# A two-layer encoder trunk on one core: expert outputs summed in DRAM instead of gathered per choice

## The reference, cut to what matters

```python
for l in range(2):
    x = x + mixer(rmsnorm(x)) @ w_out[l]
    h2 = rmsnorm(x, norm2_g[l])
    # each token: best of 4 groups, then the best 2 of that group's 4 experts, with gates
    for e in range(16):            # SwiGLU experts, 1024 -> 512 -> 1024
        act = silu(h2 @ w_gate[e]) * (h2 @ w_up[e]) * gate[:, e]
        y += act @ w_down[e]       # gate is zero for all but 2 experts of a token
    x = x + y
return rmsnorm(x, final_g)
```

## Time and profile before

| | |
|---|---|
| median of 3 runs | 1093.71 us (1092.78 to 1094.87) |
| the profiled execution's own time | 1096.58 us |
| its span, first to last instruction | 1094.3 us |
| PE busy | 1034.2 us (95%) |
| DVE, ACT, POOL busy | 549.2, 291.3, 191.8 us |
| mean granted TensorE clock | 0.987 |
| moved by DMA | 279.07 MB, mean 255 GB/s |

### The profile page before, as it was taken

How to read it: one execution, slowest core, us unless ns; L and a number is a source line. 1 busy time by engine, 2 the same in 40 slices (tenths; PEclk the granted TensorE clock), 3 DMA queues, 4 the chain that set the end, 5 groups by cost and what they waited for, 6 DMA issues and landing times.

```text
span 1094.3 us, 26585 instructions
## 1 busy us (share of the span) xinstructions
PE 1034.2 (95%) x11288; PEld 765.1 (70%) x11288; DVE 549.2 (50%) x1264; ACT 291.3 (27%) x570; POOL 191.8 (18%) x265
## 2 busy tenths in 40 slices
PE   8999998899999999899989999989999999998894
PEld 7875874587689977586578577646876778764552
DVE  5899996524711111020679999764364112102018
ACT  6225336623000100000342443465230001000013
POOL 3400000000223442322200000000003335332230
PEclk9999999999999999999999999999999999999997
DMA  9652211153999999999934122011569999999993
GB/s 358 209 230 78 77 58 39 39 193 147 394 399 406 402 404 401 405 402 400 345 125 137 53 93 89 20 51 50 202 261 401 403 406 400 404 401 407 396 389 127
DMA packets 85109, 279.07 MB, mean 255 GB/s; under 512 B 12344, under 2 KB 12448, under 8 KB 84976
## 3 DMA queue, kind: packets, MB, share of 16 engines
q1 hardware_dynamic: 69504, 237.60, 56.8%
q0 software_dynamic: 15472, 39.63, 9.8%
HBM read 257.43 MB, written 22.54 MB: 256 GB/s over the span
## 4 chain that ended last, share of the span: by engine, by line
PE 64%; DVE 16%; DMA 10%; issue 3%; ACT 3%; SPq 3%; DVEq 0%; ACTq 0%
PE ps L861 20%; PE ps L901 9%; DVE arena L1620 7%; PE ps L459 7%; PE ps L461 7%; PE ps L460 7%; DMA deep<-in_w_dn 3%; DMA deep<-in_w_gu 3%; SPq L410 3%; DVE w_lo L440 2%; PE ps L906 2%; DMA arena<-in_w_dn 2%; DVE x_sb L1559 2%; DMA arena<-in_w_gu 2%; PE ps L1048 2%
## 5 line engine op out<-in xcount | busy, mean ns | idle before, releaser
L1839 DVE SCALAR_TENSOR_TENSOR arena<-ps,gslot,arena 128x128 f32<-128x128 f32 x88 | 25.7, 345 | 368.1 <-ACT arena L1259 333.2
L861 PE MATMUL ps<-arena 128*32 128x256 f32 x2112 | 129.6, 380 | 6.3 <-DMA arena<-in_w_dn 3.2
L640 POOL DMA_INDIRECT gain<-h_rows,tab x82 | 85.1, 1037 | 231.6 <-DVE arena L1831 188.9
L459 PE MATMUL ps<-a_hi,w_hi 128*128 128x512 f32 (+1 forms) x304 | 122.5, 403 | 3.1 <-DVE w_lo L440 2.1
L460 PE MATMUL ps<-a_lo,w_hi 128*128 128x512 f32 (+1 forms) x304 | 119.3, 392 | 0.0
L461 PE MATMUL ps<-a_hi,w_lo 128*128 128x512 f32 (+1 forms) x304 | 119.2, 392 | 0.0
L861 PEld LDWEIGHTS ps<-arena 128*32 128x32 f32 x2112 | 90.4, 110 | 39.2 <-issue 9.7
L861 PE MATMUL ps<-deep,arena 128*32 128x256 f32 x1824 | 106.6, 379 | 1.0 <-DMA deep<-in_w_dn 1.0
L861 PE MATMUL ps<-raw,arena 128*32 128x256 f32 x1696 | 103.2, 379 | 0.5
L435 ACT ACTIVATE w_hi<-raw 128x1024 fp32r<-128x1024 f32 (+1 forms) x64 | 65.0, 1022 | 131.1 <-PE ps L461 130.9
L1259 ACT ACTIVATE arena<-ps 128x384 f32<-128x384 f32 (+1 forms) x32 | 14.9, 465 | 315.3 <-PE ps L861 248.8
(11 more groups left out here) (266 smaller groups left out, 1511.7 us busy)
## 6 DMA issues: line engine op xcount, KB each, us to landing
arena<-in_w_gu SPq DMA_DIRECT2D x92, 512.0 KB
deep<-in_w_gu SPq DMA_DIRECT2D x84, 512.0 KB
raw<-in_w_gu SPq DMA_DIRECT2D x80, 512.0 KB
raw<-in_w_dn SPq DMA_DIRECT2D x56, 512.0 KB
deep<-in_w_dn SPq DMA_DIRECT2D x44, 512.0 KB
raw<-in_w_in SPq DMA_DIRECT2D x40, 512.0 KB
arena<-in_w_dn SPq DMA_DIRECT2D x28, 512.0 KB
raw<-in_w_out SPq DMA_DIRECT2D x16, 512.0 KB
```

Source lines behind the costliest of these rows:

```text
L459: nc.tensor.matmul(o, lh, rh, start=start, stop=False)
L640: pool.indirect_dma_start(xg[:, s * QC:(s + 1) * QC], None, h2q[l], bass.IndirectOffsetOnAxis(ap=tab[:, s, e:e + 1], axis=0), bounds_check ...
L861: mm = T.matmul(o, rows, piece[:, :, c * P:(c + 1) * P], start=b == 0, stop=b == 7)
L1839: ins = V.scalar_tensor_tensor(out=slu[:, s, :], in0=hidden(e, 1)[:, s, :], scalar=gslot[:, s, e:e + 1], in1=slu[:, s, :], op0=ALU.mult, o ...
```

## The change

Each finished seat is added to one DRAM row per token. `ysum` has one row of 4 KB per token for each layer, cleared at the start by eight DMAs of 512 KB (with one for the zero row, nine instead of twelve). `store` issues one indirect DMA per group, three or two instead of four plain ones; the offsets are the `tab` entries that the gather used, entries out of bounds are skipped, and the DMA adds to what the row holds. Since two seats can hold the same token, each store also waits on POOL until all earlier stores have landed. At the end four plain loads of 512 KB bring the summed rows, and DVE adds four tiles instead of eight. The table of result rows `yidx[:, 0]` and the DVE instructions that made it are gone; `stored` counts indirect DMAs.

```diff
+        ysum = [nc.dram_tensor(f"y_sums{l}", (SEQ, D), F32, kind="Internal").ap() for l in range(DEPTH)]
+        ysq = [rows.rearrange("t (q n) -> (t q) n", q=4) for rows in ysum]
...
+        def stored(l, e):
+            return TURNED[STORED] * l + TURNED[e]
...
-                            sp.wait_ge(yc_in[TT - 1], 32 * l)
+                            sp.wait_ge(yc_in[TT - 1], 16 * l)
...
-                    for tile in range(1 + EXTRA):
-                        pool.dma_start(yd[ZERO_ROW + tile * P:ZERO_ROW + (tile + 1) * P, :], zeros).then_inc(y_zero, 16)
+                    pool.dma_start(yd[ZERO_ROW:ZERO_ROW + P, :], zeros).then_inc(y_zero, 16)
+                    for rows in ysum:
+                        for tt in range(TT):
+                            pool.dma_start(rows[tt * P:(tt + 1) * P, :], zeros).then_inc(y_zero, 16)
...
                 def store(e):
                     pool.wait_ge(y_set, STORED * l + e + 1)
-                    rows = yd[FIRST_ROW[e]:FIRST_ROW[e + 1], :].rearrange("(s i) (c n) -> c i s n", i=G, c=4)
-                    for c in range(4):
-                        pool.dma_start(rows[c], ysb[G * c:G * c + G, 0:GROUPS_OF[e] * QC].rearrange("i (s n) -> i s n", n=QC)).then_inc(y_stored, 16)
+                    if e:
+                        pool.wait_ge(y_stored, 16 * stored(l, e))
+                    elif l == 0:
+                        pool.wait_ge(y_zero, 16 * (1 + DEPTH * TT))
+                    for s in range(GROUPS_OF[e]):
+                        pool.indirect_dma_start(ysq[l], bass.IndirectOffsetOnAxis(ap=tab[:, s, e:e + 1], axis=0), ysb[:, s * QC:(s + 1) * QC], None,
+                                                bounds_check=4 * SEQ - 1, oob_is_err=False, compute_op=ALU.add).then_inc(y_stored, 16)
...
-                if l == 0:
-                    pool.wait_ge(y_zero, 16 * (1 + EXTRA))
-                pool.wait_ge(y_stored, 64 * STORED * (l + 1))
+                pool.wait_ge(y_stored, 16 * stored(l, STORED))
                 for tt in range(TT):
-                    for k in range(TOPE):
-                        q = TOPE * tt + k
-                        if q == LATE_FREE:
-                            pool.wait_ge(w_used, (l + 1) * PIECES_L - 8)
-                        pool.indirect_dma_start(late_rows[q], None, yd,
-                                                bass.IndirectOffsetOnAxis(ap=yidx[:, 0, k, tt:tt + 1], axis=0)).then_inc(yc_in[tt], 16)
+                    pool.dma_start(late_rows[tt], ysum[l][tt * P:(tt + 1) * P, :]).then_inc(yc_in[tt], 16)
...
-                    sc.wait_ge(y_stored, 64 * (STORED * l + e))
+                    sc.wait_ge(y_stored, 16 * stored(l, e))
...
-                ve.wait_ge(yc_in[tt], 32 * (l + 1))
-                for k in range(TOPE):
-                    ve.wait_ge(late_add, TOPE * (TT * l + tt) + k)
-                    V.tensor_tensor(x[:, tt, :], late_rows[TOPE * tt + k], x[:, tt, :], ALU.add).then_inc(late_add, 1)
+                ve.wait_ge(yc_in[tt], 16 * (l + 1))
+                V.tensor_tensor(x[:, tt, :], late_rows[tt], x[:, tt, :], ALU.add).then_inc(late_add, 1)
...
-                link(V.tensor_scalar(R["v2"], e2k[:], float(-LIGHT.start), 0.0, ALU.add, ALU.max))
...
-                V.tensor_scalar(yidx[:, 0], R["c2"], float(ZERO_ROW), None, ALU.add)
```

More of the change, by code:

```diff
@@ L76 @@
 TURNED = [sum(GROUPS_OF[:p]) for p in range(E + 1)]
-FIRST_ROW = [sum(ROWS_OF[:p]) for p in range(E + 1)]
 EXTRA = 11
@@ L80 @@
 STORED = E - LAST
-ZERO_ROW = FIRST_ROW[STORED]
+ZERO_ROW = 0
 SUM_BANK = (2, 4, 6, 0)
@@ L191, in trunk @@
         warm = sb("warm", [P, 2 + 2 * DEPTH])
-        yidx = sb("yidx", [P, 2, TOPE, TT], I32)
+        yidx = sb("yidx", [P, TOPE, TT], I32)
         e2k = sb("e2k", [P, TOPE, TT])
@@ L261, in trunk @@
         SIDE_MIX, SIDE_ROWS = 6, 10
-        late_rows = [ar(A_ACC, D), ar(A_SQ, D), *(deep[:, d].rearrange("p a n -> p (a n)") for d in (3, 7)),
-                     ar(A_L, D), ar(A_PT, D), hrow[:, TT - 1, :], ar(A_V, D)]
-        LATE_FREE = 5
+        late_rows = [ar(A_ACC, D), ar(A_SQ, D), *(deep[:, d].rearrange("p a n -> p (a n)") for d in (3, 7))]
         at = A_SC
@@ L675, in _ @@
                 with pool.If(extra > 0):
-                    pool.wait_ge(late_add, TT * TOPE * (l + 1))
+                    pool.wait_ge(late_add, TT * (l + 1))
                     pool.wait_ge(over[l].tab_step, TABLES)
@@ L690, in _ @@
                         for tt in range(TT):
-                            pool.indirect_dma_start(x[:, tt, :], None, yd, bass.IndirectOffsetOnAxis(ap=yidx[:, 1, k, tt:tt + 1], axis=0),
+                            pool.indirect_dma_start(x[:, tt, :], None, yd, bass.IndirectOffsetOnAxis(ap=yidx[:, k, tt:tt + 1], axis=0),
                                                     compute_op=ALU.add).then_inc(over[l].xg_in, 16)
@@ L1554, in add_late @@
             def add_late(l, tt):
-                ve.wait_ge(yc_in[tt], 32 * (l + 1))
-                for k in range(TOPE):
-                    ve.wait_ge(late_add, TOPE * (TT * l + tt) + k)
-                    V.tensor_tensor(x[:, tt, :], late_rows[TOPE * tt + k], x[:, tt, :], ALU.add).then_inc(late_add, 1)
+                ve.wait_ge(yc_in[tt], 16 * (l + 1))
+                V.tensor_tensor(x[:, tt, :], late_rows[tt], x[:, tt, :], ALU.add).then_inc(late_add, 1)
             def sum_ready(l, tt):
-                ve.wait_ge(late_add, TOPE * (TT * l + tt + 1))
+                ve.wait_ge(late_add, TT * l + tt + 1)
                 ve.wait_ge(ysum_ready, TT * l + tt + 1)
@@ L1745, in extras @@
                     link(V.scalar_tensor_tensor(out=R["ex"], in0=R["count"], scalar=float(q), in1=R["ex"], op0=ALU.is_gt, op1=ALU.add))
-                link(V.tensor_scalar(R["v2"], e2k[:], float(-LIGHT.start), 0.0, ALU.add, ALU.max))
[L1747 to L1753, removed]
                 link(V.tensor_tensor_scan(R["cum"], cst[:, C_ONE:C_ONE + E], R["ex"], 0.0, ALU.mult, ALU.add))
-                link(V.scalar_tensor_tensor(out=R["c2"], in0=R["k2"], scalar=float(CAP), in1=R["c2"], op0=ALU.is_lt, op1=ALU.mult))
                 V.tensor_tensor(first_of[:], R["cum"], R["ex"], ALU.subtract)
                 V.tensor_copy(ovx[:, EXTRA:EXTRA + 1], R["cum"][:, E - 1:E])
-                link(V.scalar_tensor_tensor(out=R["c2"], in0=R["b2"], scalar=float(-ZERO_ROW), in1=R["c2"], op0=ALU.add, op1=ALU.mult))
-                V.tensor_scalar(yidx[:, 0], R["c2"], float(ZERO_ROW), None, ALU.add)
                 link(V.tensor_tensor(R["cmp"], R["cum"].unsqueeze(1).to_broadcast([P, EXTRA, E]),
@@ L1802, in over_rows @@
                 step(V.scalar_tensor_tensor(out=R["d2"], in0=R["b2"], scalar=float(OVER_ROW - ZERO_ROW - E * P), in1=R["d2"], op0=ALU.add, op1=ALU.mult))
-                V.tensor_scalar(yidx[:, 1], R["d2"], float(ZERO_ROW), None, ALU.add)
+                V.tensor_scalar(yidx[:], R["d2"], float(ZERO_ROW), None, ALU.add)
                 for k in range(TOPE):
@@ L1927, in _ @@
                 if l == 0:
-                    ve.wait_ge(y_zero, 16 * (1 + EXTRA))
+                    ve.wait_ge(y_zero, 16 * (1 + DEPTH * TT))
                 for v, (h, b) in enumerate(DOTS):
```

## The result

The changed kernel takes 1101.85 us (median of 6 runs, 1098.94 to 1104.14), the kernel before 1094.82 us in the same comparison (6 runs, 1092.78 to 1096.51): ratio 1.006, 95% interval [1.0045, 1.0075]. It is 7.0 us slower where 6.1 us less was forecast. The profiled execution took 1102.13 us with a span of 1100.2 us; the granted clock was 0.99, the same as before.

What follows compares the result with a forecast made beforehand. It took the DMA engines to bound the expert stages and DVE the layer ends; -7.2 us at the ends and +1.1 us for adding stores gave -6.1 us, 1093.71 becoming 1087.6 us, range 1079 to 1107.

Steps and rivals of the forecast that it cites:

- What bounds the kernel: Expert stages up to seat 13's last down weights: DMA engines set the pace, 2.49 us per MB paid nearly one for one.
- The ends of the layers: Last `last_y` to first `add_sum`: fewer DVE additions save 3.1 us in the first layer, 4.1 in the second, 7.2 together.
- Filled slots and bytes: Stores of seats 0 to 12: skipped slots move nothing, so 3.26 and 3.15 MB per layer instead of 4.59.
- The price of an added megabyte: Expert-stage stores: an added megabyte costs m times a copied one; m=1.5 taken, together +1.1 us.
- The break-even: Price of adding in the expert-stage stores at which the change gains nothing: m=1.9.
- (a): Rival, expert-stage stores: an addition costs two copies, m about 2, +1.9 us, 1095.6 us; chance 0.23.
- (c): Rival, expert-stage stores: slow addition, each packet waits for its DRAM row, m of 3, +17.8 us, 1111.5 us; chance 0.17.
- the signs it had named as wrong: DVE waiting for the late loads, ACT waiting for stores, or expert-stage stretches longer by over 4 us.
- GpSimd's issues: Expert-stage stores: three indirect issues at 1.04 us and two gaps take 3.7 us against 2.20, at no cost in time.
- ACT's wait for landed stores: ACT's next copy into the one tile `ysb`: stores land just in time; no cost up to a landing of 12 us.
- `extras` and the rest: Fewer `extras` instructions, SP's waits, zero stores and late rows: 0, at most 1.8 us per layer for `extras`.
- (e): Rival, indirect stores: empty slots not skipped, 4.59 MB per layer counts, 1097.9 us; chance 0.08 together with another rival.

Runs made afterwards that it cites:

- e6: The kernel before with each plain store issued twice, the second time to another DRAM tensor: 1116.58 us, ratio 1.023.
- s1: The changed kernel with GpSimd made to wait about 1 us after every gather: 1100.89 us, ratio 1.0055.
- s2: The kernel before with the first tile's two additions ahead of the first `last_y` and GpSimd waiting about 1 us after every gather: 1094.86 us, ratio 0.9992.
- e2: The kernel before with only the layer ends changed: four plain loads (not the tokens' rows) for eight gathers, and four additions: 1086.8 us, ratio 0.9914.
- s4: The kernel of c1 with GpSimd made to wait about 1 us after every gather and every store: 1090.41 us, ratio 0.995.
- e1: The changed kernel with indirect stores that write instead of adding, in both layers: 1706.37 us, ratio 1.559.
- s3: The kernel of e5 with GpSimd waiting about 1 us after every gather and, in the second layer, every store: 1092.57 us, ratio 0.9979.
- e5: The changed kernel, adding in the first layer and only writing in the second: 1120.11 us, ratio 1.0238.
- e3: The changed kernel with a second result tile for two seats, so ACT need not wait for the store just issued: 1102.34 us, ratio 1.0053.
- c1: Against the kernel before: one DRAM row per token's choice, indirect stores without adding, eight plain loads, eight additions (two tiles' ahead of first `last_y`): 1137.43 us, ratio 1.039.

## Why the prediction was wrong

- **What bounds the kernel.** Right for the stage as a whole. e6 paid 2.36 us for a copied MB against 2.49 assumed, and taking PE's pauses away (s1, s2) changed nothing. Its early seats go at PE's pace, which the prediction did not say.
- **The ends of the layers.** Right. 3.1 and 4.1 us were forecast, 3.4 and 4.4 measured, by the mechanism described, with DVE waiting for ACT. The late loads were 0.85 us late once, in the first layer, where the prediction had taken no wait. One thing it took as given: in the second layer of the kernel before, ACT's first copies begin 3.5 us after PE's last weight load for them (1063.75 to 1067.21), while GpSimd issues the eight gathers; in the changed kernel and in e2 it is 0.9 us. Had they come after 0.9 us there too, DVE's chain would have reached `add_sum` some 1.7 us earlier, by an estimate from the durations in the earlier trace rows, if the late rows were there. So part of the 4.4 us may be owed to the gathers that are gone and not to fewer additions; no run takes this apart.
- **Filled slots and bytes.** Right. The router's 3.26 and 3.15 MB at the price of a copy give the stages of s4 to 0.3 us against the one profile of before, which is closer than those profiles repeat (1.8 us).
- **The price of an added megabyte: the step that failed.** "I take m=1.5", because copies overlap read and write. Measured: 2.3 by the engines' shares (e1 against the changed kernel, s3 against s1), 2.1 to 2.4 by the times of s1 and s3, and 2.27 and 2.33 from the stages of the changed kernel against before, ((6.96/2.49) + 4.59)/3.26 and ((6.85/2.49) + 4.59)/3.15 (2.4 and 2.3 with the mean stages of all profiles). With m=2.3 the prediction's own sum is (3.26×2.3 - 4.59 + 3.15×2.3 - 4.59)×2.49 = +13.9, less 7.2: +6.7 us; measured +7.0. The break-even was put at 1.9, so the kernel ended on the other side of it, between rivals (a) and (c), whose 1095.6 and 1111.5 us enclose 1101.85. Two of the signs it had named as wrong came: ACT waits for stores, and both stages are longer by over 4 us. The reason I gave (overlap) is not borne out: the engines were already full (share 1.03), and with the additions they deliver 384 GB/s, not 403, so what an addition takes is missing elsewhere. What inside an engine takes the time is not shown; the packets in the same window are 6720 against 3448.

  The Trainium skill (Collectives: The Full Stack, stop 4 and the part on why ReduceScatter is half of AllGather) has two source reads and half the rate for the adding step of a collective. That gives m=2, nearer than my value. The engines' shares here, 2.3, are above it, and the measurement decides; the times alone (2.1 to 2.4) would not tell the two apart.
- **GpSimd's issues.** Wrong, harmless: 1.58 us for an adding issue where 1.04 was assumed. The longer spacing may even have helped: the adding stores at 857.70 to 861.47 leave PE without a pause, where e5's stores 1.3 us apart do not.
- **ACT's wait for landed stores.** Wrong, harmless in the changed kernel: 63.1 us of waits where none were expected, and no time when 48 of them were taken away (e3). I take it that PE had this slack because its weights are late anyway; that was not tried by itself. In s1 and s3, with the issues apart, the same wait does stop PE, for 3.5 and 2.8 us in the second stage.
- **`extras` and the rest.** Valued at 0. The ledger has -0.8 and +0.7 us for them, less than these rows vary from run to run; nothing speaks against 0.
- **Empty slots not skipped (e).** Refuted: with full slots GpSimd's queue would have moved the 9.07 MB of before in the window from 272 to 500 us; it moved 7.45.

## What to carry to other kernels

Under a stage in which the DMA engines are full, price a transfer in engine time and not in bytes: here an adding store cost about 2.3 copies, so it pays only where it replaces more than that many bytes of copies, and skipping 30% of the slots did not. Separate the parts of such a change: the four additions less at the end were worth 9 us (e2), skipping the empty slots with indirect stores that don't add some 2 to 4 us per layer (s4), and the addition itself cost 8 to 11 us per layer (s1 against s3). And look at how closely GpSimd issues indirect transfers before you call a slower variant refuted: the same kernel was 4% slower than before with the issues 1.3 us apart (c1) and 0.5% faster with them 2.5 us apart (s4).

## What the runs showed of the hardware

- An adding indirect store takes GpSimd 1.58 us to issue, the same store without adding 1.00 us, and in the first stage's window (272 to 500 us) the queue needed 6720 packets against 3448 and 13.7% of the engines against 8.5%, for 7.45 and 7.07 MB (changed kernel, e1).
- When GpSimd issues indirect transfers 1.3 us apart, gathers or stores, PE pauses from about the third on, mostly 0.55 to 0.6 us at a time with a few weight loads between, until the row of issues ends: a seat with four of them is 2.3 us longer (e5, c1). Three adding stores 1.9 us apart show none (changed kernel, 857.70 to 861.47), nor do issues 2.5 us apart (s3). The granted clock in the stretches with pauses was 1.00 (e5 and c1). What on the chip links the two is open; the runs show that the spacing decides, not what path it takes.
- Such pauses cost nothing while the engines bind (s1, s2) and 27.5 us when they have made room (e5, s3).
